# Multiplying the inverse root mean square of x onto the results of the first projection, in a one-core decoder kernel

## The reference

```python
def rmsnorm(x, g):
    r = x32 * lax.rsqrt(jnp.mean(x32 * x32, axis=-1, keepdims=True) + EPS)
    return (r * g.astype(jnp.float32)).astype(x.dtype)
...
h = rmsnorm(x, g_mix[i])
proj = h @ w_in[i]
x_r, g_r, q, k, v, gate_r, gate_a = jnp.split(proj, IN_SPLIT_POINTS, axis=-1)
```

## Time and profile before

| what | value |
|---|---|
| time, median of 3 runs | 2995.91 us (2995.71 to 2996.25) |
| the profiled execution: its own time | 2994.97 us |
| its span, first to last instruction | 2993.2 us |
| mean granted TensorE clock, as a share of full speed | 0.989 |
| TensorE busy | 2910.4 us (97%) |
| VectorE busy | 2132.3 us (71%) |
| ScalarE busy | 1411.0 us (47%) |
| GpSimd busy | 425.6 us (14%) |

### The profile page before, as it was taken

The page is one execution under the profiler, slowest core; times in us unless marked ns, Lnnn a source line. Parts: engine busy times, 40 slices in busy tenths (PEclk is TensorE's granted clock), DMA queues, the critical chain, the costliest instruction groups (busy, mean ns, idle before and its releaser), DMA issues.

```text
span 2993.2 us, 45154 instructions
## 1 busy us (share of the span) xinstructions
PE 2910.4 (97%) x16516; PEld 2526.9 (84%) x16516; DVE 2132.3 (71%) x2372; ACT 1411.0 (47%) x1671; POOL 425.6 (14%) x382
## 2 busy tenths in 40 slices
PE   7999999999999999999999999999999997999997
PEld 6888888888888888888888888888888886888786
DVE  6666656776676677766666667876887776788777
ACT  5666643346644444443343344544444545434553
POOL 1000000203010000000000000116921100980110
PEclk9999999999999999999999999999999998999998
DMA  5545556653455566666565665566554554555453
GB/s 182 163 148 167 162 179 192 200 188 111 125 188 187 187 195 202 186 195 190 176 187 176 198 190 182 182 193 182 169 181 149 162 178 132 176 170 185 132 168 113
DMA packets 516869, 518.39 MB, mean 173 GB/s; under 512 B 17425, under 2 KB 514685, under 8 KB 516733
## 3 DMA queue, kind: packets, MB, share of 16 engines
q1 hardware_dynamic: 512357, 508.32, 54.2%
q0 software_dynamic: 3296, 5.56, 0.7%
q10 hardware_dynamic: 1080, 2.69, 0.3%
HBM read 514.39 MB, written 2.12 MB: 173 GB/s over the span
## 4 chain that ended last, share of the span: by engine, by line
PE 58%; DVE 9%; ACT 3%; issue 2%; DMA 0%; POOL 0%; DVEq 0%; ACTq 0%; POOLq 0%
PE PG L1753 37%; PE PG L1756 18%; DVE WL L1065 3%; ACT WH L594 1%; DVE G L1078 1%; DVE MIX L1507 1%; DVE G L1293 0%; DVE TT L1235 0%; DVE XRES L1606 0%; DVE TT L1618 0%; PE PX L1802 0%; ACT YH L685 0%; DVE F L1078 0%; PE PX L1900 0%; PE PX L1909 0%
## 5 line engine op out<-in xcount | busy, mean ns | idle before, releaser
L1753 PE MATMUL PG<-XH,WH 128*128 128x512 f32 x4864 | 1550.6, 400 | 36.2 <-DVE XH L1090 23.3
L1065 DVE TENSOR_TENSOR WL<-RAW,WH 128x1024 fp32r<-128x1024 f32 (+1 forms) x944 | 1130.8, 1231 | 444.1 <-ACT WH L594 433.9
L594 ACT ACTIVATE WH<-RAW 128x1024 fp32r<-128x1024 f32 (+1 forms) x972 | 991.9, 1049 | 772.3 <-PE PG L1756 536.5
L1756 PEld LDWEIGHTS PG<-XH,WL 128*128 128x128 f32 x4864 | 918.3, 189 | 217.5
L1756 PE MATMUL PG<-XH,WL 128*128 128x256 f32 x4864 | 959.9, 279 | 0.0
L1753 PE MATMUL PG<-YH,WH 128*128 128x512 f32 x2848 | 898.5, 397 | 6.7 <-DVE YH L1090 3.7
L1753 PEld LDWEIGHTS PG<-XH,WH 128*128 128x128 f32 x4864 | 747.9, 190 | 52.5 <-issue 41.6
L1756 PEld LDWEIGHTS PG<-YH,WL 128*128 128x128 f32 x2848 | 535.0, 188 | 126.4
L1756 PE MATMUL PG<-YH,WL 128*128 128x256 f32 x2848 | 559.6, 278 | 0.0
L1753 PEld LDWEIGHTS PG<-YH,WH 128*128 128x128 f32 x2848 | 434.2, 189 | 11.2 <-issue 9.6
L1078 DVE TENSOR_REDUCE G<-PG 128x512 f32<-128x1024 f32 x198 | 241.2, 1218 | 33.7 <-PE PG L1756 33.6
(11 more groups left out here) (261 smaller groups left out, 1499.2 us busy)
## 6 DMA issues: line engine op xcount, KB each, us to landing
RAW<-in_w_in_dram SPq DMA_DIRECT2D x488, 512.0 KB, 4.7
RAW<-in_w_ffn_gu_dram SPq DMA_DIRECT2D x176, 512.0 KB, 4.6
RAW<-in_w_ffn_down_dram SPq DMA_DIRECT2D x88, 512.0 KB, 4.6
RAW<-in_w_out_dram SPq DMA_DIRECT2D x64, 512.0 KB, 4.7
RAW<-in_w_rnn_out_dram SPq DMA_DIRECT2D x40, 512.0 KB, 4.6
RAW<-in_w_attn_out_dram SPq DMA_DIRECT2D x32, 512.0 KB, 4.5
RAW<-in_w_o_dram SPq DMA_DIRECT2D x32, 512.0 KB, 4.8
RAW<-in_w_ple_gate_dram SPq DMA_DIRECT2D x32, 512.0 KB, 4.8
```

The lines of the kernel that those rows point to most:

```text
L594: nc.scalar.activation(WH[:, u % SLOTS, 0:nk, :], RAW[:, u % SLOTS, 0:nk, :], ACT.Copy)\
L1065: V_.tensor_tensor(WL[:, u % SLOTS, 0:nk, :], RAW[:, u % SLOTS, 0:nk, :], WH[:, u % SLOTS, 0:nk, :].bitcast(fp), ALU.subtract).then_inc(s. ...
L1753: mm(PG[:, 2 * par + j, :], WH[:, slot, kk, P * j:P * j + P], x, start=grp.opens and n == 0 and kk == 0, stop=False)
L1756: last = mm(PG[:, 2 * par + j, T:2 * T], WL[:, slot, kk, P * j:P * j + P], x[:, 0:T], start=False, stop=grp.closes and n == len(units) - 1 ...
```

## The change

x comes in four DMAs of 512 KB. TensorE transposes it into `PX`, and both halves of `XH` are made straight from there: ScalarE writes the high part as x times the gain (`first_high`), VectorE the low part (`first_low`), which also copies x into `XRES`. The inverse root is left out of `XH`. It is computed later (`first_squares`, `first_inverse`, `first_diagonal`), spread by TensorE behind the first group (`rows_of_inverse`), kept in a new tile `RINV`, and multiplied onto the results of all 62 groups of `w_in`, in `evacuate`, ahead of the signal `evac`. The low parts of the first group's weights go from GpSimd to VectorE. SP issues the first unit's weights at once and holds the next three back until the third quarter of x is in. The transposes of the last quarter stand on TensorE behind the first unit of the first group.

```diff
@@ VectorE, evacuate
-                V_.reduce_sum(out, PG[:, 2 * par:2 * par + 2, :].rearrange("p b (h t) -> p b t h", h=2), AX)\
-                    .then_inc(s.evac, 1)
+                ins = V_.reduce_sum(out, PG[:, 2 * par:2 * par + 2, :].rearrange("p b (h t) -> p b t h", h=2), AX)
+                if grp.W is w_in:
+                    done(ins)
+                    ins = V_.tensor_tensor(out, out, RINV[:, :].unsqueeze(1).broadcast_to([P, 2, T]), ALU.mult)
+                ins.then_inc(s.evac, 1)
@@ ScalarE
+            def first_high(h):
+                for q in (2 * h, 2 * h + 1):
+                    act.wait_ge(s.tp, q + 1)
+                    if q == 0:
+                        from_dve()
+                    for e in range(2):
+                        last = nc.scalar.activation(XH[:, 2 * q + e, 0:T], PX[:, q % 4, T * e:T * e + T], ACT.Copy,
+                                                    scale=vec("g_mix", 2 * q + e))
+                    last.then_inc(s.act, 1)
                     act.wait_ge(s.act, c.next("act"))
...
                     if later:
-                        split(grp)
                         for h in range(DC // UK):
-                            norm(h)
+                            split(grp, slice(h, h + 1))
+                            first_high(h)
+                            if h < 2:
+                                last = first_squares(h)
+                        first_inverse(last)
@@ VectorE
+            def first_low(h):
...
                 for q in (2 * h, 2 * h + 1):
+                    from_act()
                     for e in range(2):
...
+                        ins = V_.scalar_tensor_tensor(XH[:, ch, T:2 * T], PX[:, q % 4, T * e:T * e + T],
+                                                      vec("g_mix", ch), XH[:, ch, 0:T].bitcast(fp),
+                                                      ALU.mult, ALU.subtract)
+                    ins.then_inc(s.op, 1)
+                    dve.wait_ge(s.op, c.next("op"))
+                    V_.tensor_copy(pair(XRES, q), two(PX[:, q % 4, :])).then_inc(s.tpd, 1)
...
                         for h in range(DC // UK):
-                            norm(h)
-                        c.add("unit", SLOTS)
-                        dve.wait_ge(s.lo, SLOTS)
+                            first_low(h)
+                            split(grp, slice(h, h + 1))
+                        first_diagonal()
@@ SyncE
-            sp.wait_ge(s.x_in0, 16)
...
+                    if c.n.get("unit", 0) == 1:
+                        sp.wait_ge(s.x_in2, 16)
```

More of the change, by code:

```diff
@@ L393, in program @@
                  "op",
[L394 removed]
+                 "x_in0", "x_in1", "x_in2", "x_in3", "mats", "g_in", "vecs", "lam", "keep", "p_in", "tab", "strip", "tb", "out",
                  "tp",
@@ L951, in _ @@
             act.dma_start(MATS[:, :], A["c_mats"]).then_inc(s.mats, 16)
[L952 to L956, removed]
+            for h in range(4):
+                part = slice(D // 4 * h, D // 4 * (h + 1))
+                act.dma_start(F[:, 0:NB * D].rearrange("p (b d) -> p b d", b=NB)[:, :, part],
+                              A["x"][0].rearrange("(b p) d -> p b d", p=P)[:, :, part]).then_inc(x_sems[h], 16)
             act.wait_ge(s.mats, 16)
             preload_ln()
[L960 to L973, removed]
             c.add("ss")
@@ L1294, in over_rms, with first_diagonal, first_rows @@
                 dve.wait_ge(s.dve, c.next("dve"))
-            def norm(h):
+            def first_low(h):
                 if h == 0:
-                    dve.wait_ge(s.ss, c.next("ss"))
-                    done(V_.tensor_copy(Gf[:, 0, T:2 * T], PX[:, 0, 0:T]))
+                    dve.wait_ge(s.tp, 1)
+                    V_.tensor_copy(VEC[:, 0:DC], PG[:, 3, 0:DC]).then_inc(s.dve, 1)
+                    dve.wait_ge(s.dve, c.next("dve"))
                 for q in (2 * h, 2 * h + 1):
+                    from_act()
                     for e in range(2):
[L1302 to L1308, removed]
+                        ch = 2 * q + e
+                        ins = V_.scalar_tensor_tensor(XH[:, ch, T:2 * T], PX[:, q % 4, T * e:T * e + T],
[4 more added lines that the diff above has]
+                    V_.tensor_copy(pair(XRES, q), two(PX[:, q % 4, :])).then_inc(s.tpd, 1)
+                    dve.wait_ge(s.tpd, c.next("tpd"))
+            def first_diagonal():
+                inverse_root(der(D_MS, NB), der(D_R, NB), der(D_SS, NB))
+                for b in range(NB):
+                    ins = V_.tensor_scalar(Gf[:, 1, P * b:P * b + P], IDENT, der(D_R + b), None, ALU.mult)
+                ins.then_inc(s.ready, 1)
+                dve.wait_ge(s.ready, c.next("ready"))
+            def first_rows():
+                dve.wait_ge(s.ss, c.next("ss"))
+                done(V_.tensor_copy(RINV[:, :], PX[:, 0, 0:T]))
             def bias_strip():
@@ L1625, in ln @@
                     low(XH, 7, pair(XRES, 7))
[L1628 to L1639, removed]
             def derive():
@@ L1710, in _ @@
                         split(grp, slice(UK - 1, UK))
-                    pending = [lambda fn=fn, grp=grp, j=j: fn(grp, 0, j)] + later
+                    pending = ([first_rows] if later else []) + [lambda fn=fn, grp=grp, j=j: fn(grp, 0, j)] + later
                     later = []
@@ L1804, in heads_out, with rows_of_inverse @@
                 last.then_inc(tell, 1)
+            def rows_of_inverse():
+                ready()
+                for b in range(NB):
+                    last = mm(PX[:, 0, P * b:P * b + P], ONES, Gf[:, 1, P * b:P * b + P], start=True, stop=True)
+                last.then_inc(s.ss, 1)
             def vectors():
                 pe.wait_ge(s.vecs, 16 * VEC_DMAS)
+                pe.wait_ge(s.tpd, DC // 2)
                 for t in range(VEC_TILES):
@@ L2005, in _, with last_transposes @@
                         src = D * b + P * (2 * q + e)
-                        last = nc.tensor.transpose(PG[:, q % 4, at:at + P], Fv[:, src:src + P], IDENT)
+                        last = nc.tensor.transpose(PX[:, q % 4, at:at + P], Fv[:, src:src + P], IDENT)
                 last.then_inc(s.tp, 1)
-                if q == 7:
-                    ready()
-                    for b in range(NB):
-                        last = mm(PX[:, 0, P * b:P * b + P], ONES, Gf[:, 1, P * b:P * b + P], start=True, stop=True)
-                    last.then_inc(s.ss, 1)
+            def last_transposes():
+                first_transposes(6)
+                first_transposes(7)
+            pe.wait_ge(s.mats, 16)
+            pe.wait_ge(s.g_in, 16)
+            nc.tensor.transpose(PG[:, 3, 0:DC], RT[0:DC, 0:P], IDENT[0:DC, 0:DC])
+            for q in range(6):
+                first_transposes(q)
             for ph in phases:
@@ L2021, in turn @@
                         first = isinstance(i, int) and i == 0
-                        group(grp, ph.fresh.get(j, ()) if first else (),
-                              {0: diff_sum} if j == 1 and ph.name[:4] == "outa" else None)
+                        mid = {0: diff_sum} if j == 1 and ph.name[:4] == "outa" else None
+                        if first and j == 0 and ph.name == "attn":
+                            mid = {0: last_transposes}
+                        group(grp, ph.fresh.get(j, ()) if first else (), mid)
                         if hook:
```

36 lines of the change are left out of this document (23 added, 13 removed).

## The result

The kernel before takes 2995.85 us (median, 2993.70 to 2996.64), the changed one 3000.27 us (2997.38 to 3004.08), each from 20 runs; the ratio is 1.0016, 95% interval [1.0009, 1.0023]. The change costs 4.4 us, 0.15%. No change lies outside the interval, so it is slower; the 0.2% named in the prediction lies inside the interval, above the measured value. The profiled execution of the changed kernel takes 3000.95 us (span 2999.1), 6.0 more than the one before.

The account below looks back on a forecast made before the run. TensorE was taken to set the pace from 28 to 800 us, VectorE in `g_r`. 2994.97 - 3.4 (start) + 0.1 (slack) + 11.7 (late) = 3003.3 us profiled, 3004.2 us as median; range 2997 to 3009.

Parts of the forecast that it names:

- What the start gains: Kernel start: first reduce near 38.7 us instead of 43.51, 4.8 us won; fourth group 3.4 us earlier after two multiplications.
- The two multiplications in the first groups: First groups, on VectorE's chain: each multiplication costs 0.73 us, taken off the 4.8 us won at the start.
- `attn`, gates, `x_r` hide theirs: 40 to 800 us: VectorE's idle time covers 0.73 us per group, tightest `x_r` with 0.95 us; loss taken as 0.
- `gate_r` gives 3.4: `gate_r`: first two steps hide their 0.73 us, the third gives 0.44, the next four all; 3.4 us by 805.48.
- 12 multiplications behind it, less 0.5, 8.3: Last `gate_r` job and eleven of `g_r`: 12 x 0.73 = 8.8 us lost, 0.4 to 0.5 swallowed behind `g_r`.
- The two rules: Skill page on VectorE: 65 ns more per PSUM read (sum 3005.4); minimize chained operations, waits free (sum 3003.5).
- the late stretch hides nothing: Judges the rival that `gate_r` and `g_r` hide the multiplication in VectorE's idle time: 2992.6 or 2989.4 us, chance 0.10.
- The start gives something: Judges the rival that the start gives nothing because held-back weights arrive late: 3007.6 us, chance 0.12.
- The clock does not fall in each round of `g_r`: Judges the rival that added waits of some 1.3 us in `g_r` cost TensorE its clock; chance 0.04.
- A single fall: Clock rival's size: one group at half speed costs 11 us more, so a single one gives 3015 us.
- Cheaper late, better start: Rival: `gate_r` gives little, late loss 8 to 9.5 us, start gains 5 to 6; about 3000 us, chance 0.22.
- The signs: Expected in the changed kernel's trace: TensorE's first units, `g_r` periods 12.3 us, waits some 19 us, `rnn_out` 8 us later.

Follow-up runs that it names:

- e1: The changed kernel without any of its 62 multiplications by the inverse root; 2989.81 us, ratio 0.9984.
- e7: The changed kernel with the multiplication of every first-projection result done twice; 3031.26 us, ratio 1.0122.
- e4: The kernel before with GpSimd's memset of reused gate strips (last 8 of 16) cut to one column; 2994.31 us, ratio 0.9998.
- e5: The changed kernel with the multiplication left out in `g_r` alone; 2994.26 us, ratio 0.9996.
- e3: The kernel before, old start kept, with each of the 62 first-projection results multiplied by ones after its reduce; 3007.57 us, ratio 1.004.
- e8: The changed kernel with the softplus of `lru_lambda` moved from behind the first group to behind the 29th and 30th; 2996.98 us, ratio 1.0007.
- e6: The changed kernel multiplying only in `attn` and `gate_a`, later input remade with the inverse root during `attn_out`, softplus behind groups 29 and 30; 2988.16 us, ratio 0.9976.

## Why the prediction was right, and where it was off

Forecast 3004.2 (2997 to 3009), measured 3000.27. For the profiled execution the sum was 3003.3 and 3000.95 came. The direction and the mechanism held, and the range, but the chances did not fit as well: 0.52 lay on 3001.9 to 3006, which did not come, 0.68 on slower by over 0.2%, and the loss is 0.15%. The sum lay only 2.3 us above that line and was 3.9 too high. Of these, 1.6 are luck of the executions: the profiled one of the kernel before lay 0.9 under its median, that of the changed one 0.7 above. The other 2.4, in the trace, are 1.0 at the start, 0.6 late, and 0.8 in the last stages, which the change doesn't explain. The 0.6 is itself two errors that partly cancel, 1.1 too much for `gate_r` and 0.5 too little behind it.

- *What the start gains* (first reduce at 38.7, the fourth group 3.4 less a slack of 0.1): 36.76 and 4.3. Two terms were mis-sized. Unit 1 was ready for ScalarE at 13.79, not 15.0: its load started with x's third quarter in at about 9.7, and took 4.1 us and not 4.7. The chain from there was right in its parts: two L1323 0.88 (0.90 said), a copy 0.69 (0.71), a quarter with split 4.5 (4.55); it ended at 29.28 (31.2), and the reduce came 2 us earlier. What I did not see is that TensorE would then stand for 2.6 us ahead of the third group, lose its clock, and give 1.1 us back. From the third group's start to the fourth's the prediction took VectorE's 11.5 us to be the longer way; TensorE took 13.15 us there, and 11.68 in e1.
- *The two multiplications in the first groups*: 1.5 us said; e1 and the changed kernel differ by 2.58, of which 1.1 is that clock and 0.4 the earlier first reduce, so about 1.1 is left for the two.
- *`attn`, gates, `x_r` hide theirs*: right: TensorE has no wait from 65 to 700 us, and no kernel but e7 drifts in the table by over 0.4 us from the fourth group to `gate_r`. But the cover of 0.95 us, read at one place of `x_r`, was nearly spent: 0.12 us is left per group.
- *`gate_r` gives 3.4*: 2.3 by the first start of `g_r`, because the multiplication shifted two copies out of a memset, worth 0.43 and 0.58 us. e4 shows that cause.
- *12 multiplications behind it, less 0.5, 8.3*: 1.0 for the job of the last `gate_r` result and 7.6 for `g_r` (e5), with 0.2 for e5's slightly later start 8.8. Late 11.1 against 11.7.
- *The two rules*: L1323 reads PSUM and takes 0.88 us for two, no more than L1302 out of SBUF alone, 1.80 us for four. The extra latency for PSUM in the Trainium skill, "VectorE: DVE Perf Modes", section "The TRN2 errata — SBUF-src ops pay a fixed extra latency per instruction", is not seen. That page's "Rules for kernel authors" speaks against longer chains, and this case agrees: 0.73 us for each link where VectorE sets the pace, 0.03 to 0.04 of it the wait.
- *The rivals*: the late stretch hides nothing (e3). The start gives something (e3 against the changed kernel, 7.3 us). The clock does not fall in each round of `g_r`: with waits of 0.8 to 1.1 us the changed kernel keeps 1.00 from 840 to 940 us. It fell in the wait of 7.4 us at the head of `g_r`, as before in the one of 5.4 (both have 0.57 over the 8 us from there), behind 2.57 us at 48 and behind 1.80 us at 832. A single fall was priced at 11 us, a whole group at half speed; the one at 48 us cost 1.1, the one at 832 nothing: e8 has no fall there and loses the same 8.8 us from the first start of `g_r` on. The loop of which the Trainium skill tells in "TensorE: Matmul & The Clock Gate", section "HAM oscillation", waits for DMAs in each round for longer than it computes; the groups of `g_r` wait 1 us in 12, so the prediction read more into it than it says, and no run here tests it. "Cheaper late, better start" gave the right time, about 3000, by a wrong share: it wanted 5 to 6 us from the start and a late loss of 8 to 9.5, and 4.3 and 11.1 came.
- *The signs*: TensorE's first two units began at 14.02 and 20.16 us (15 and 21.5 said), the periods of `g_r` have 12.35 us in the mean (12.3), TensorE's waits from 700 to 950 us sum to 15.5 (some 19), and `rnn_out` comes 6.8 us later (8).

## What to carry to other kernels

Moving a factor from an input to the results trades one short serial stretch for a cost per result; price it stage by stage, by who sets the pace there. Room for a cost that recurs was, in `x_r`, the second engine's waiting time per period and not the lead that its output had; in `attn` another chain of waits was tighter still. And a front that comes earlier can hit the next serial piece, here a parameter derivation, 10 us from the reduce to the next split: look what TensorE will find there, since a wait can cost the clock behind it as well.

## What the hardware showed unexpectedly

- VectorE's copy of 128x256 takes 0.29 us alone and 0.87 to 1.03 us beside GpSimd's memset of 128x1024, which takes its 0.95 to 0.97 us all the same. Each slowed copy ends 0.15 us behind the memset, so what it loses depends on when it starts: the change moved two copies by 0.4 and 0.7 us against the memsets, and that was worth 1.0 us.
- Behind a wait of 2.57 us TensorE was granted 0.57 from 48 to 52 us, so it ran at half clock (1.2 GHz) for most of it; behind one of 1.7 us at the same place (e1) it kept 2.4 GHz. Behind 1.80 us at 832 the changed kernel was granted 0.83 from 830 to 840 us, while e8, with 1.81 us at the same group, kept 1.00 (825 to 835 us). In `conf1` every kernel waits 1.8 to 1.9 us at the same group, and three (e3, e4, e6) lose their clock. Length alone does not decide it in these rows.
- A fall cost 1.1 us at 48 us, where TensorE set the pace by then, 1.6 us in `conf1`, and nothing that the starts show at 832 us, where VectorE set it.
